# Start of a two-block kernel reordered: x and later weight chunks held until memory has landed, x's squares later, forget gates' logits on four column tiles

## The reference

```python
mod = silu(c) @ w_ada + b_ada                       # 1024 -> 3 * 1024
shift, scale, gate = split(mod, 3)
h = rms_norm(x, g_pre) * (1 + scale) + shift
qa, ka, va, fa, za, qb, kb, vb, zb = split(h @ w_in)     # fa has 8 columns, one per head
cum = cumsum(log_sigmoid(fa + b_fgate))             # forgetting attention's bias
oa = softmax(qa @ ka.T / 8 + cum_q - cum_k, causal) @ va * silu(za)
ob = sliding_window_attention(rope(qb), rope(kb), vb, sinks) * silu(zb)
x = x + gate * rms_norm(concat(oa, ob) @ w_out, g_post)
# block 2: convolution, differential attention, and cross attention to a memory of 256 rows
k, v = split(rms_norm(mem, mem_g) @ w_mem_kv)       # needs nothing of block 1
```

## Time and profile before

| | |
|---|---|
| median of 3 runs (lowest to highest) | 1152.31 us (1152.17 to 1152.65) |
| the profiled execution's own time | 1153.57 us |
| its span, first to last instruction | 1151.8 us |
| busy: PE, PEld, DVE, ACT, POOL | 98%, 80%, 71%, 51%, 6% |
| chain that ended last: PE, DVE, ACT, DMA, issue | 89%, 5%, 3%, 2%, 2% |
| mean granted clock of TensorE | 0.996 |
| read from HBM | 121.59 MB |

### The profile page before, as it was taken

How to read it: one execution, slowest core, us unless ns; L and a number is a source line. 1 busy time by engine, 2 the same in 40 slices (tenths; PEclk the granted TensorE clock), 3 DMA queues, 4 the chain that set the end, 5 groups by cost and what they waited for, 6 DMA issues and landing times.

```text
span 1151.8 us, 15721 instructions
## 1 busy us (share of the span) xinstructions
PE 1124.1 (98%) x5796; PEld 919.5 (80%) x5796; DVE 819.5 (71%) x1424; ACT 585.8 (51%) x1084; POOL 66.2 (6%) x73
## 2 busy tenths in 40 slices
PE   5899999999999999999999999999999999999998
PEld 5898777766898877877778778888888888788887
DVE  5788655668566347999999985898777787853342
ACT  6663555456565455766766663325553223651230
POOL 2019500101000000000000000000000000000000
PEclk9899999999999999999999999999999999999999
DMA  9967422321355322212222242323223333223221
GB/s 343 353 218 256 128 72 74 92 65 38 129 169 197 109 75 73 74 38 92 74 92 74 72 145 96 110 77 106 74 74 98 123 98 104 92 73 110 93 72 73
DMA packets 35276, 130.20 MB, mean 113 GB/s; under 512 B 4272, under 2 KB 4656, under 8 KB 34688
## 3 DMA queue, kind: packets, MB, share of 16 engines
q1 hardware_dynamic: 31536, 112.74, 29.3%
q0 software_dynamic: 3376, 16.23, 4.2%
q10 hardware_dynamic: 288, 0.24, 0.1%
HBM read 121.59 MB, written 6.29 MB: 111 GB/s over the span
## 4 chain that ended last, share of the span: by engine, by line
PE 89%; DVE 5%; ACT 3%; DMA 2%; issue 2%; SPq 0%; POOL 0%; DVEq 0%; ACTq 0%
PE bank L475 27%; PE bank L477 26%; PE bank L476 26%; PE bank L726 2%; PE bank L577 2%; DMA raw<-in_chunks 2%; PE bank L847 2%; PE bank L754 1%; DVE wl L1813 1%; PE bank L680 1%; ACT qf L1211 1%; DVE stat L1969 0%; DVE cumt L2502 0%; ACT wh L1130 0%; PE bank L716 0%
## 5 line engine op out<-in xcount | busy, mean ns | idle before, releaser
L475 PE MATMUL bank<-hl,wh 128*128 128x512 f32 x888 | 357.9, 403 | 0.0
L477 PE MATMUL bank<-hh,wh 128*128 128x512 f32 x888 | 347.0, 391 | 0.0
L476 PE MATMUL bank<-hh,wl 128*128 128x512 f32 x888 | 346.2, 390 | 0.0
L1813 DVE TENSOR_TENSOR wl<-raw,wh 128x1024 fp32r<-128x1024 f32 x185 | 225.1, 1238 | 103.8 <-ACT wh L1130 103.0
L1130 ACT ACTIVATE wh<-raw 128x1024 fp32r<-128x1024 f32 x185 | 192.0, 1058 | 205.8 <-PE bank L477 186.3
L475 PEld LDWEIGHTS bank<-hl,wh 128*128 128x128 f32 x888 | 167.1, 188 | 36.6 <-issue 3.1
L477 PEld LDWEIGHTS bank<-hh,wh 128*128 128x128 f32 x888 | 166.7, 188 | 36.2
L476 PEld LDWEIGHTS bank<-hh,wl 128*128 128x128 f32 x888 | 167.2, 188 | 31.3 <-issue 0.7
L2225 DVE SCALAR_TENSOR_TENSOR ca<-u,vt,ca 128x512 f32<-128x512 f32 x232 | 157.9, 746 | 0.0
L476 PE MATMUL bank<-oh,wl 128*128 128x512 f32 (+1 forms) x256 | 94.0, 367 | 0.0
L477 PE MATMUL bank<-oh,wh 128*128 128x512 f32 (+1 forms) x256 | 93.9, 367 | 0.0
(11 more groups left out here) (337 smaller groups left out, 1649.1 us busy)
## 6 DMA issues: line engine op xcount, KB each, us to landing
raw<-in_chunks SPq DMA_DIRECT2D x193, 512.0 KB, 3.6
ada_a<-in_chunks SPq DMA_DIRECT2D x8, 512.0 KB, 11.6
ada_b<-in_chunks SPq DMA_DIRECT2D x8, 512.0 KB, 9.5
x<-in_x POOLq DMA_DIRECT2D x4, 512.0 KB, 10.5
mem_scratch<-kvm POOLq DMA_DIRECT2D x1, 2048.0 KB, 9.5
x<-in_x POOLq DMA_DIRECT2D x1, 2048.0 KB, 8.5
x_scratch<-x POOLq DMA_DIRECT2D x1, 2048.0 KB, 7.7
kvm<-mem_scratch POOLq DMA_DIRECT2D x1, 2048.0 KB, 9.3
```

What stands on the lines that cost most here:

```text
L475: pe.matmul(o, a[0], b[1], start=start, stop=False, **kw)
L476: pe.matmul(o, a[1], b[0], start=False, stop=False, **kw)
L477: return pe.matmul(o, a[0], b[0], start=False, stop=stop, **kw)
L1813: dve.tensor_tensor(wl[:, w], raw[:, RAW_SLOT[nxt]], wh[:, w].bitcast(F32), ALU.subtract)\
```

## The change

- SyncE waits for memory's landing before mk1's load; GpSimd waits for it before x's. The first 16 pieces each wait for the landing of the third piece before (the first three for mk1, mk2, mk3). The pieces begin behind mk3 instead of mk1.
- ScalarE squares memory's first tile, VectorE its second. Only mk0 is split before memory's transposes, not mk1.
- x's squares go from before the first pair of mk to behind it (two tiles) and behind the second pair (two, and the root). VectorE normalises x at the third pair, behind `ahead`, instead of the first.
- The chunk fa is gone. The gates' 8 columns (padded to 32) are loaded as plain f32, and `gate_logits` multiplies them by h (plain f32, `xT`) in eight matmuls: column tile k takes features 256k to 256k + 255. ScalarE copies the bank, and one f32 matmul with the pattern `fours` adds the four partial sums after va's first step. The bias and the logarithms follow there on VectorE and ScalarE, with `ahead` calls between, and ScalarE's wait for the store goes ahead of them. `sel`'s load waits for the logits' bank, since it lies where `xT` lies.

```diff
@@ -65,7 +66,7 @@
 CHUNKS = [("mk", j) for j in range(8)] + [("mv", j) for j in range(8)]
-CHUNKS += [("fa", 0), ("qa", 0)] + [("va", j) for j in range(4)] + [("ka", 0)]
+CHUNKS += [("qa", 0)] + [("va", j) for j in range(4)] + [("ka", 0)]
@@ -182,7 +184,7 @@
 ADA_SLOTS, ADA_EARLY = 8, 16
-ADA_BEHIND = (0, 2, 1, 2, 1, 1, 1, 1, 1, 1, 1, 1, 2, 1, 0, 0, 0, 2, 0, 2, 0, 2, 0, 2)
+ADA_BEHIND = (0, 0, 0, 2, 1, 2, 1, 2, 1, 2, 1, 2, 1, 1, 0, 0, 0, 2, 0, 2, 0, 2, 0, 2)
@@ -239,7 +242,9 @@
            "dkn": "diff_kn_g_2", "subln": "diff_subln_g_2", "xqn": "x_qn_g_2", "xkn": "x_kn_g_2"}
-    vt = np.zeros((P, VT_COLS), np.float32)
+    vt = np.zeros((P, VT_COLS + 32 * C), np.float32)
+    gates = np.asarray(inputs["w_in"])[0][:, 1536:1544].reshape(C, P, 8)
+    vt[:, VT_COLS:].reshape(P, C, 32)[:, :, 0:8] = gates.transpose(1, 0, 2)
@@ -273,10 +278,6 @@
             a = w_out_2[:, cols]
-        elif kind == "fa":
-            a = np.zeros((D, P), np.float32)
-            for part in range(4):
-                a[:, 32 * part:32 * part + 8] = w_in[:, 1536:1544]
@@ -377,7 +378,8 @@
         ident_b = sb("ident_b", [P, P], BF16)
-        dist, blocks, xk = shared([("dist", [P, S], F32), ("blocks", [P, P], F32)], [("xk", [P, 2, 2, MEM], F32R)])
+        dist, blocks, fours, fgate, xk = shared([("dist", [P, S], F32), ("blocks", [P, P], F32), ("fours", [P, P], F32),
+                                     ("fgate", [P, C, 32], F32)], [("xk", [P, 2, 2, MEM], F32R)])
@@ -643,9 +645,27 @@
-            chunk(("fa", 0), H, split=s.h_lo)
-            chunk(("qa", 0), H)
-            wide("va", 0, H, [(tt, (2, 3, 4, 7)[tt]) for tt in range(T)])
+            def gate_logits():
+                pe.wait_ge(s.fours_in, 32)
+                b = next_bank()
+                banks.open(pe, b, "fa")
+                for i in range(2):
+                    for part in range(4):
+                        c, rows = 2 * part + i, slice(32 * part, 32 * part + 32)
+                        ins = pe.matmul(ps[b][rows, :], fgate[:, c, :], xT[:, c], start=i == 0, stop=i == 1,
+                                        skip_group_check=True)
+                banks.close(ins, "fa")
+            chunk(("qa", 0), H, split=s.h_lo)
+            gate_logits()
+            tiles = [(tt, (2, 3, 4, 7)[tt]) for tt in range(T)]
+            for s_ in range(4):
+                if s_ == 1:
+                    banks.wait_empty(pe, "fa")
+                    banks.open(pe, 6, "logits")
+                    banks.close(pe.matmul(ps[6][:], fours[:], cumt[:, 1, :], start=True, stop=True), "logits")
+                used(wide_step("va", 0, s_, H, tiles), "va", 0, s_, tiles)
@@ -1012,6 +1032,10 @@
                         sp.wait_ge(s.w_lo, NCH[last] + 1)
+                if name == ("mk", 1):
+                    sp.wait_ge(s.mem_in, 16 * 2)
+                if name[0] == "ada" and name[1] < ADA_EARLY:
+                    wait_raw(sp, ("ada", name[1] - 3) if name[1] > 2 else ("mk", name[1] + 1))
@@ -1025,11 +1049,14 @@
         def _(pool):
+            pool.wait_ge(s.mem_in, 16 * 2)
...
                 pool.dma_start(lam4[:, n, :], t[name].partition_broadcast(P)).then_inc(s.bcast_in, 16)
+            pool.dma_start(fours[:], t["consts"][:, K_FOURS:K_FOURS + P]).then_inc(s.fours_in, 16)
+            pool.dma_start(fgate[:].rearrange("p c n -> p (c n)"), t["vectors"][:, VT_COLS:]).then_inc(s.fours_in, 16)
@@ -1040,6 +1067,7 @@
             pool.wait_ge(s.h_lo, 8)
+            banks.wait_full(pool, "fa")
@@ -1213,16 +1241,17 @@
             act.dma_start(cst[:], t["consts"][:, 0:K_ONES]).then_inc(s.const_in, 16)
-            act.dma_start(vt[:], t["vectors"]).then_inc(s.rows_in, 16)
+            act.dma_start(vt[:], t["vectors"][:, 0:VT_COLS]).then_inc(s.rows_in, 16)
...
             act.wait_ge(s.mem_in, 16 * 2)
-            square_rows(memx, MEM_SS, 2)
-            act.wait_ge(s.sumsq, 2)
+            square_rows(memx, MEM_SS, 1)
+            act.wait_ge(s.sumsq, 1)
+            act.wait_ge(s.mem_squared, 1)
...
             act.activation(tc_, v8("c"), ACT.Tanh, scale=0.5).then_inc(s.c_tanh, 1)
-            ahead(None, 2)
+            ahead(None, 1)
@@ -1230,10 +1259,6 @@
             ahead(None)
-            act.wait_ge(s.x_in, 16 * T)
-            square_rows(x, X_SS, T)
-            act.wait_ge(s.sumsq, 6)
-            act.activation(X_SS, X_SS, ACT.Sqrt, scale=1.0 / D, bias=eps6).then_inc(s.small_sqrt, 1)
@@ -1259,6 +1284,12 @@
                 ahead(("mk", 2 * h + 1))
+                if h < 2:
+                    act.wait_ge(s.x_in, 16 * T)
+                    square_rows(x[:, 2 * h:2 * h + 2], X_SS[:, 2 * h:2 * h + 2], 2)
+                if h == 1:
+                    act.wait_ge(s.sumsq, 5)
+                    act.activation(X_SS, X_SS, ACT.Sqrt, scale=1.0 / D, bias=eps6).then_inc(s.small_sqrt, 1)
@@ -1281,16 +1312,6 @@
-            act.wait_ge(s.cum_dve, 1)
-            f, e, l, cum = (cumt[:, n, :] for n in range(4))
-            act.activation(e, f, ACT.Abs).then_inc(s.cum_act, 1)
-            act.wait_ge(s.cum_act, 1)
-            act.activation(e, e, ACT.Exp, scale=-1.0).then_inc(s.cum_act, 1)
-            act.wait_ge(s.cum_act, 2)
-            act.wait_ge(s.ones_in, 16)
-            act.activation(e, e, ACT.Ln, bias=ones[:, 0:1]).then_inc(s.cum_act, 1)
-            ahead(("fa", 0))
@@ -1299,7 +1320,7 @@
-            raw_q(("qa", 0), 0, 0)
+            raw_q(("qa", 0), 0, 0, False)
@@ -1321,11 +1342,23 @@
             split_q(0)
+            f, e, l, cum = (cumt[:, n, :] for n in range(4))
+            banks.wait_full(act, "fa")
+            banks.empty(act.activation(e, ps[banks.where["fa"][0]][:], ACT.Copy), "fa")
+            ahead(("qa", 0))
             act.wait_ge(s.kvm_out, 16)
+            ahead(("va", 0))
+            act.wait_ge(s.cum_dve, 1)
+            act.activation(e, f, ACT.Abs).then_inc(s.cum_act, 1)
+            act.wait_ge(s.cum_act, 1)
+            act.activation(e, e, ACT.Exp, scale=-1.0).then_inc(s.cum_act, 1)
+            act.wait_ge(s.cum_act, 2)
+            act.wait_ge(s.ones_in, 16)
+            act.activation(e, e, ACT.Ln, bias=ones[:, 0:1]).then_inc(s.cum_act, 1)
+            ahead(("va", 1))
...
             act.activation(negcum[:], cum, ACT.Copy, scale=-1.0).then_inc(s.cum_hi, 1)
-            for s_ in range(3):
-                ahead(("va", s_))
+            ahead(("va", 2))
@@ -1820,6 +1853,9 @@
             dve.memset(eps5, 1e-5).then_inc(s.eps_done, 1)
+            dve.wait_ge(s.mem_in, 16 * 2)
+            dve.tensor_tensor_reduce(macc[:, 0, :], memx[:, 1, :], memx[:, 1, :], 1.0, 0.0, ALU.mult, ALU.add,
+                                     MEM_SS[:, 1:2]).then_inc(s.mem_squared, 1)
@@ -1846,7 +1882,7 @@
                 ahead(("mk", 2 * h + 1))
-                if h == 0:
+                if h == 2:
@@ -1892,15 +1928,6 @@
             f, e, l, cum = (cumt[:, n, :] for n in range(4))
-            key = ("fa", 0)
-            banks.wait_full(dve, key)
-            banks.empty(dve.tensor_scalar(f, bank(key)[:], fbias, None, ALU.add), key)
-            banks.wait_empty(dve, key)
-            dve.memset(l, 1.0).then_inc(s.cum_dve, 1)
-            ahead(key)
-            dve.wait_ge(s.cum_act, 3)
-            then(dve.scalar_tensor_tensor(e, f, 0.0, e, ALU.min, ALU.subtract))
-            dve.tensor_tensor_scan(cum, l, e, 0.0, ALU.mult, ALU.add).then_inc(s.cum_dve, 1)
@@ -1919,6 +1946,15 @@
             split_q(0, 1)
+            ahead(("va", 0))
+            banks.wait_full(dve, "logits")
+            banks.empty(dve.tensor_scalar(f, bank("logits")[:], fbias, None, ALU.add), "logits")
+            banks.wait_empty(dve, "logits")
+            dve.memset(l, 1.0).then_inc(s.cum_dve, 1)
+            dve.wait_ge(s.cum_act, 3)
+            then(dve.scalar_tensor_tensor(e, f, 0.0, e, ALU.min, ALU.subtract))
+            dve.tensor_tensor_scan(cum, l, e, 0.0, ALU.mult, ALU.add).then_inc(s.cum_dve, 1)
+            ahead(("va", 1))
```

More of the change, by code:

```diff
@@ L52 @@
 K_DIST = 385 + 4 * P
-K_COLS = K_DIST + S
+K_FOURS = K_DIST + S
+K_COLS = K_FOURS + P
 VEC_ROWS = [("c", 8), ("b_ada", 16), ("g_pre", 8), ("norm_g", 8), ("mem_g", 8), ("dw_b", 8), ("ln_g", 8),
@@ L146 @@
 SIGNALS = {
-    "ones_in": "ones loaded", "sq_hi": "differential outputs' squares: hi", "sq_lo": "lo",
+    "ones_in": "ones loaded", "fours_in": "forget gates' weights and the pattern that adds four partial sums loaded",
+    "sq_hi": "differential outputs' squares: hi", "sq_lo": "lo",
     "const_in": "identity and frequencies loaded", "rows_in": "packed vectors loaded",
     "tables_in": "masks, distances and blocks loaded",
-    "mem_in": "memory loaded", "x_in": "x loaded", "bcast_in": "lambdas and sinks loaded on every partition", "late_in": "positions, gate bias and gain",
+    "mem_in": "memory loaded", "mem_squared": "squares of the memory's second tile added up", "x_in": "x loaded", "bcast_in": "lambdas and sinks loaded on every partition", "late_in": "positions, gate bias and gain",
```

(7 more changed lines are left out.)

## The result

| | before | after |
|---|---|---|
| median of the comparison (lowest to highest) | 1152.24 us (1151.31 to 1152.65, 4 runs) | 1168.43 us (1167.72 to 1170.37, 4 runs) |
| span of the profiled execution (own time) | 1151.8 us (1153.57) | 1165.9 us (1167.72) |
| TensorE busy, mean granted clock | 1124.1 us, 0.996 | 1124.4 us, 0.988 |

What follows compares the result with a forecast made beforehand. TensorE, busy for 98% of the span, was taken to bound the kernel unless it waits. Terms +1.0 + 2.5 + 0.6 + 0.7 = +4.8 gave 1157.1 us, range over the cases 1148.5 to 1161.5.

Steps and rivals of the forecast that it cites:

- x's transposes (xn's chain): At x's transposes: TensorE waits for VectorE's xn, there at 50.1 against 49.12, +1.0 us (-2.3 to +2.5).
- clock behind that idling, to mv3's end: After TensorE's wait of about 9 us for xn: half clock costs 2.5 us (0 to 3.4).
- gate's matmuls, counted from mv3's end: Forget gates: their matmuls wait for the last pieces, starting 38.7 us after mv3's end instead of 38.1, +0.6 (-2.8 to +1.5).
- clock behind it: At the gate's matmuls: TensorE's idling of 3.4 us can halve the clock again, 0.7 us (0 to 1.7).
- weight slots shifted by one: From the output projection on: slots shift by one, TensorE covered but for waits below 1.5 us, 0 (-1 to +1).
- the gate's matmuls start at 38.7: After mv3's end: store's landing at 17.4 plus a chain of 21.3 us, where TensorE is ready at 35.3.
- The landing: GpSimd's store of memory's keys and values, ahead of the gate: lands 8.6 us after issue (7.7 to 9.5).
- The issue: GpSimd's store after mv3's end: issued after qa0 5.44, logits 1.75 and three issues of 0.54 = 1.6 us.
- The chain behind the landing: From the store's landing to the gate's matmuls: high half, low halves, pieces, scan and other steps, 21.3 us.
- The column tiles: Forget gates' logits: eight f32 matmuls run four abreast in two rounds, 1.75 us in all.
- The hold of x: At the start: holding x until memory has landed gives memory 0.35 us, 0.6 at most.
- The chains are shorter: Rival at xn and gate: xn at 46.8, clock costs +1.3, pieces in time; -3.8, 1148.5 us; chance 0.22.
- Column tiles in less than four: Rival at the logits: the eight take 3.5 or 6.9 us; 1158.9 to 1162.2 us; chance 0.12.

Runs made afterwards that it cites:

- e6: Changed kernel with the store of memory's keys and values issued first on GpSimd, ahead of sel, masks and the logits' bank wait: 1161.47 us, ratio 1.0074.
- e4: Changed kernel with ScalarE's wait for the store moved from ahead of ka0's high half to ahead of va's copies: 1162.19 us, ratio 1.0079.
- e5: Changed kernel with the last four pairs of modulation pieces loaded and worked one chunk earlier: 1161.11 us, ratio 1.0067.
- e12: Changed kernel with the store still behind the logits' bank wait, but ahead of sel and the masks: 1166.43 us, ratio 1.012.
- e10: e7 without the hold of x (its four loads issued at once), second chunk still held behind memory: 1150.24 us, ratio 0.9979.
- e7: Changed kernel with four moves: xn first, ScalarE's store wait late, last pieces one chunk earlier, store first on GpSimd: 1151.72 us, ratio 0.9987.
- e9: e7 with the modulation piece behind mv0's low half moved behind mv2's: 1149.58 us, ratio 0.9972.
- e8: Kernel before with only the logits as column tiles, plus late store wait, pieces one chunk earlier and store first: 1152.18 us, ratio 1.0.
- e1: Kernel before with only the changed start; chunk fa and the full chunk of logits kept: 1159.0 us, ratio 1.0048.
- e2: Changed kernel with its start put back, so only the forget gates' edits remain: 1162.12 us, ratio 1.0081.
- e11: Changed kernel with three moves at the gate (store wait late, pieces one chunk earlier, store first), start as changed: 1160.69 us, ratio 1.0067.
- e3: Changed kernel with VectorE normalising x at the third pair ahead of mv0's and mv1's low halves: 1161.11 us, ratio 1.0066.

## Why the forecast was right in sign and short by 11 us

Position by position (us; the first four measured ones add up to the 14.0 at the first scores, the fifth comes behind them):

| step of the prediction | forecast | measured |
|---|---|---|
| x's transposes (xn's chain) | +1.0 (-2.3 to +2.5) | +2.3 |
| clock behind that idling, to mv3's end | +2.5 (0 to 3.4) | +2.8 |
| gate's matmuls, counted from mv3's end | +0.6 (-2.8 to +1.5) | +6.6 |
| clock behind it | +0.7 (0 to 1.7) | +2.3 |
| weight slots shifted by one | 0 (-1 to +1) | +1.05 |

**The step that failed is the third: "the gate's matmuls start at 38.7".** Its mechanism was right in every link, and e6, e4 and e5 show one link each: GpSimd's store behind the logits' bank, ScalarE's wait for it, the last pieces behind VectorE's queue. Three of its sizes were too small:

* *The landing.* I took 8.6 us between two stores of 2 MB in the page, with 9.5 as the far end. It took 12.1. A landing is no property of the store: the queues were full and it waited for what was on them. The change itself put 384 KB right ahead of it, and moved it to a moment when it shares them with more of SyncE's loads (e6, e12). +3.5.
* *The issue.* The logits' bank reached GpSimd 2.7 us after the first of their matmuls, not 1.75, and qa0 took 5.56: +1.1.
* *The chain behind the landing.* 22.7 instead of 21.3: the pieces cost 1.93 each, not 1.72, and the low halves 1.85, not 1.75, all of them beside GpSimd's arithmetic. +1.4.

A stall that was forecast with 3.4 us was 8.8, and the clock behind it fell for longer, 10.2 us: that is the fourth line, 1.6 over.

**x's chain** held link by link. Mk5's high half started at 26.01 (forecast landing 25.7), and VectorE's part took 8.81 us for 8.8. ScalarE's part ended 1.3 late, 0.9 of it a wait for mk7, which landed at 33.79. TensorE idled 9.2 us for the 9 forecast. That the wait came out so close is in part luck: xn was 1.3 us late, and TensorE itself was ready at 42.2, 1.2 later than the 41 forecast.

**The column tiles** were right: 1.92 us for the eight, where one after the other they would take 8 x 0.86 = 6.9 us, 3.6 times as long. The Trainium skill's "TensorE: Matmul & The Clock Gate", section "Part 3: Packing small matmuls — row/col tiling", gives 2.38 times for three tiles; by an estimate from that figure the eight would have taken 2.9 us. The trace has them, on four tiles, at 1.92, so the estimate was too high here.

**The hold of x** was priced at 0.35 us, and memory landed 0.39 earlier (6.26 for 6.65; 0.2 in e10). Over all profiled kernels it landed at 6.13 to 6.46 in the ten with the hold and at 6.57 to 6.73 in the four without. The Trainium skill's "DMA: Bandwidth & Descriptors", section "Issuing engines are not separate DMA queues", says that such DMAs interleave on the same 16 engines. The estimate of over 1 us that the prediction worked out from this alone does not come true here.

**The rivals.** "The chains are shorter" asked for the pieces within 36 us of mv3's end and for xn by 46; e7, e9 and e10 have both (35.7, and xn by 43.4), and they are not slower than before; e8, with the start of before and the gate at 36.4, is level. "Column tiles in less than four" is excluded by the row. What none of them held is that the stall could be more than twice the forecast, because my range for the landing came from two durations measured under other traffic. That the sign was right owes nothing to the size of the stall: x's chain and its clock alone, 5.1 us, gave it (e1).

**What stays open.** The half clock behind the modulation lasted 3.4 us in some executions and 6.8 in others (69.8 to 73.2 before, 74.5 to 77.9 after, 71.7 to 78.6 in e6, 64.8 to 71.7 in e7), with the same instructions in front of it. In all fourteen profiled executions it is the long one where the clock fell 2.3 to 2.9 us after the first of the one-column matmuls, and the short one where it fell 3.7 to 5.0 after. No run here says what decides, and it is worth 1.7 us each time.

The fifth line of the table comes from a wait that the kernel before does not have, for VectorE's probabilities, after and in e9:

```profile
283.94 0.66 PE L746 MATMUL bank<-cst,prob 128*128 128x128 f32 x4 [1.11 <-DVE prob L2027]
```

```profile
265.95 0.66 PE L746 MATMUL bank<-cst,prob 128*128 128x128 f32 x4 [1.89 <-DVE prob L2026]
```

In the changed kernel ScalarE and VectorE split a chunk at 276.6 and 277.8, ahead of these probabilities. All twelve kernels without the chunk fa lose 1.05 us or more here, and e1, which keeps it, loses nothing; that fits the shift of the weight slots, which the prediction put at nothing (between -1 and +1), but no run undid that shift alone. In e2, e6, e9, e11 and e12 the wait was 1.9 to 2.4 us, a half clock of 3.4 or 6.8 us came with it, and 3.2 to 3.9 us were lost, against 1.05 to 1.35 in the other seven. So the first scores of e9 came 6.2 us earlier than before and its span is only 2.2 shorter; its profiled execution (1151.46) lies 1.9 over its median, and whether the others had this half clock too is not shown. Here lie 1.1 of the 1.6 us that e7 lost of the 3.4 it had won at the first scores.

## What to carry to other kernels

Time a transfer in the middle of a kernel by the bytes that will be on the queues with it, at the rate the windows show, and not by the landing that the same transfer had elsewhere. When several engines hand one thing on (issue, landing, copy, low half, piece), one link moved out of the chain can be worth nearly as much as all of them: here the gate moved from 44.7 to 36.3 us behind mv3's end with e5 alone and to 35.7 with all three. Find first what the engine at the end needs by itself, here 35.7 us. Where work is dropped from a list by which other work is placed, look at what slides: with the modulation's last pieces moved back by the one chunk, and nothing else, the ratio fell from 1.0145 to 1.0067 (e5).

## What the runs showed that I had not expected

* A wait of TensorE of some 9 us came with half clock for 10 to 14 us, part of it still in the wait (43.8 to 57.4 and 125.7 to 135.9, after). So it costs more than itself: 2.8 us behind the first, 2.3 behind the second. Most waits of 1.7 to 2.8 us came with a half clock too, of 3.4 or 6.8 us (e3, e4, e7, e8, e10, and the five at the probabilities), but e5's 2.15 us in front of the scores did not.
* Four f32 column tiles of 32 columns run side by side, each four starting 7 ns apart: 16 instructions in 1.92 us, which is what two full-width matmuls take (1.88).
* The same store of 2 MB (memory's keys and values) took 8.3 to 12.4 us in the fourteen profiled kernels; the four that were looked at differ by what shared the queues with it.
